# Spreading seven routing steps over later row blocks in a fused MoE and attention kernel

## The chip, the cores and the metric

The kernel runs on one core of one Trainium2 chip. The metric is the device time of one execution in microseconds (us). Three executions of the kernel before took 2537.6, 2530.3 and 2535.9 us; their median is 2535.9 us.

## The reference

Two transformer blocks run one after the other on 512 tokens of width 1024. The first has a convolution mixer and then a layer of 16384 experts. For each token and each of 8 heads the layer finds the 16 best experts (two top-16 searches over 128 scores each, then a top-16 over the 256 sums of the winners), and each chosen expert is one row of `u` (a dot product with the token) and one row of `v` (added to the token, weighted):

```python
v1, i1 = lax.top_k(s1, 16)
v2, i2 = lax.top_k(s2, 16)
cand = (v1[..., :, None] + v2[..., None, :])
vals, pos = lax.top_k(cand, 16)
idx = i1[pos // 16] * 128 + i2[pos % 16]
gates = softmax(vals)
act = gelu(einsum("chkd,cd->chk", u[idx], xc))
out = einsum("chk,chkd->cd", act * gates, v[idx])
```

The second block is: a feed-forward layer (hidden width 2816), two attention mixers over the same tokens with gated outputs, and a second feed-forward layer.

## The kernel before, in words

**Rows.** The tokens lie in 4 tiles of 128. A "row" of the kernel is one expert choice for one tile: 4 tiles x 8 heads x 16 choices = 512 rows. For a row, GpSimd issues a gather (L2104) that brings one `u` row and one `v` row for each of the 128 tokens into one of 7 pair buffers (1 MB). VectorE makes the dot product (`dot`, L1519), ScalarE the gelu and the weight (L1593). The `v` half is added in one of two ways: for most of rows 0 to 263 by a diagonal matmul on TensorE (L551), and for all rows from 264 on by VectorE (`add_row`, L963, two rows behind the dot). A buffer is free for the gather of row i when row i - 7 has been added.

**Blocks and routing.** 16 rows, those of one tile and one head, are a block, n = 0 to 31. The indices and gates of a block come from `route(n)` on VectorE: 21 pieces (three top-16 searches, the sums, the decoding of positions), which a Python generator hands out, 4 pieces after each row's dot and add, so that one route is spread over 6 rows. `ROUTES[n]` lists which routes are made while block n's rows are worked on. A second route of a block begins 8 rows after the first. After a route, ScalarE takes its exponentials (`gates(r)`, three instructions), six rows after the route's first. There are 16 slots for finished routes. GpSimd waits for route n before the first gather of block n.

**Chains.** Tiles 0 and 1 are ready after row 255. From then on the whole second block of the model for these 256 tokens ("chain A") is worked on beside rows 256 to 511; TensorE has nothing else from row 264 on. Chain A's stages are a norm, feed-forward 1 (22 weight chunks up, 12 down), a norm, the projections (`lat`, `fq`, `fk`, `fv`), 32 attention steps (`look`, `turn`, `prep`), the gates and branches, a norm, and feed-forward 2. After row 511 the same second block follows for tiles 2 and 3 ("chain B").

**Order.** Every engine works in program order. On VectorE, ScalarE and GpSimd the steps of chain A are put between the rows by a fixed table: `clock(i)` gives each row a time (`PACE`, L98), each step of the chain has a planned time, and behind row i come the steps that are due. A step that is not yet ready so holds up the rows behind it on its engine. VectorE's loop is

```python
for n in range(32):
    for k in range(16):
        if k % 8 == ROUTE_AT[n]:
            steps = route(ROUTES[n][k // 8]) if k // 8 < len(ROUTES[n]) else iter(())
        i = 16 * n + k
        dot(i)
        if i >= 2 and not ON_PE[i - 2]:
            add_row(i - 2)
        for _ in range(4):
            next(steps, None)
        ...
        first.until(clock(i))
```

Weights come in chunks of up to 1 MB through three buffers, issued by SyncE; a buffer is filled again when TensorE has used it.

Of the kernel before, what the change touches and what calls it, by code (L numbers as in the profile page):

```python
# [114 lines left out]
ON_PE = [i < HALF + 8 and not (i < 128 and i % 4 == 3) for i in range(PAIRS)]  # L115

ROUTES, SLOTS = [], 16
for _k in [1] * 8 + [2] * 8 + [1, 2, 1, 2, 1] + [0] * 11:
    _at = 1 + sum(len(r) for r in ROUTES)
    ROUTES.append(list(range(_at, _at + _k)))  # L120

ROUTE_AT = [2 if _n < 8 else 0 for _n in range(32)]
UP_TO = [(sum(ON_PE[:i]), i - sum(ON_PE[:i])) for i in range(PAIRS + 1)]
# [2121 lines left out]
```

## Time and profile before

| | |
|---|---|
| median of 3 runs | 2535.9 us |
| profiled execution, time | 2537.6 us |
| profiled execution, span of its instructions | 2535.8 us |
| TensorE busy | 84% |
| VectorE busy | 71% |
| ScalarE busy | 46% |
| GpSimd busy | 29% |
| HBM traffic | 760.86 MB, 300 GB/s on average |

Busy shares are averages over stages of very different kinds. From about 250 to 1870 us the rows are worked on, from 965 us together with chain A; from 1876 us to the end chain B runs alone.

### The profile page before, as it was taken

The numbers are of one execution on the slowest core, as the hardware profiler recorded it, in microseconds if no ns is written. First come the engines' busy times: TensorE is split into PE (matmuls) and PEld (weight loads), VectorE is DVE, ScalarE is ACT, GpSimd is POOL, SyncE is SP. The second block draws the span as 40 slices with busy tenths as digits, with TensorE's granted clock in tenths as the row PEclk, the third lists the DMA queues.
The fourth block names the chain that finished last, engine by engine and source line by source line (L and its number), as shares of the span: only waits on it lengthen the run. The fifth ranks groups of instructions, "written<-read, shape, count | busy, mean of one in ns | idle before, by whom it ended". The sixth has DMA issues, their size and how long they took to land.

```text
span 2535.8 us, 28491 instructions
## 1 busy us (share of the span) xinstructions
PE 2139.5 (84%) x9496; PEld 1516.8 (60%) x9496; DVE 1812.1 (71%) x3312; ACT 1178.1 (46%) x3774; POOL 745.8 (29%) x634
## 2 busy tenths in 40 slices
PE   6987898988777778998755697999739989998999
PEld 6965443433222227873434484786339977797997
DVE  6975767778888887888898968675665546546454
ACT  5224555656666664432455543333244435344442
POOL 0002344454554543233555533332310002000000
PEclk9988999999999998999866598999969989799999
DMA  5112999999999998999998999999945542124453
GB/s 208 67 67 97 392 390 413 412 421 421 421 421 420 416 408 343 399 420 395 370 364 319 369 420 421 376 421 421 378 188 188 185 148 88 67 99 167 160 189 133
DMA packets 107458, 760.86 MB, mean 300 GB/s; under 512 B 12064, under 2 KB 12832, under 8 KB 16432
## 3 DMA queue, kind: packets, MB, share of 16 engines
q0 software_dynamic: 73728, 536.90, 52.1%
q1 hardware_dynamic: 33584, 222.15, 23.1%
q8 instruction: 75, 1.23, 0.2%
q14 instruction: 71, 0.58, 0.1%
HBM read 756.91 MB, written 2.10 MB: 299 GB/s over the span
## 4 chain that ended last, share of the span: by engine, by line
PE 42%; DVE 9%; DMA 5%; issue 3%; ACT 2%; POOL 1%; DVEq 0%; ACTq 0%
PE bank L551 41%; DMA pair<-in_uv,idx 5%; DVE resid L963 4%; DVE pair L1519 2%; DVE half L957 1%; DVE tmp L957 1%; PE bank L923 0%; PE bank L571 0%; ACT frow L1593 0%; ACT half L1593 0%; DVE smalls L1236 0%; POOL pair L2104 0%; DVE smalls L1309 0%; POOL smalls L2059 0%; DVE ft_lo L957 0%
## 5 line engine op out<-in xcount | busy, mean ns | idle before, releaser
L2104 POOL DMA_INDIRECT pair<-in_uv,idx x512 | 641.7, 1253 | 901.5 <-DVE resid L963 573.1
L1593 ACT ACTIVATE smalls<-smalls 128x1 f32<-128x1 f32 x2058 | 540.2, 286 | 669.3 <-DVE smalls L1519 651.0
L1519 DVE CUSTOM_DVE_ANT_0 pair<-pair,hn 128x1024 f32<-128x1024 f32 x512 | 623.5, 1219 | 174.8 <-DMA pair<-in_uv,idx 173.1
L551 PE MATMUL bank<-pair,diag 128*128 128x512 f32 x928 | 459.3, 627 | 120.2 <-ACT diag L1593 119.4
L551 PEld LDWEIGHTS bank<-pair,diag 128*128 128x128 f32 x928 | 168.5, 194 | 392.7 <-ACT diag L1593 247.1
L551 PE MATMUL bank<-ft,raw 128*128 128x256 f32 x1664 | 365.7, 383 | 11.9 <-DVE ft L957 11.9
L963 DVE SCALAR_TENSOR_TENSOR resid<-pair,smalls,resid 128x1024 f32<-128x1024 f32 x280 | 358.1, 1279 | 0.6 <-ACT smalls L1593 0.3
L551 PEld LDWEIGHTS bank<-ft,raw 128*128 128x128 f32 x1664 | 320.3, 193 | 57.2 <-issue 12.7
L957 DVE TENSOR_TENSOR half<-raw,half 128x1024 fp32r<-128x1024 f32 (+1 forms) x204 | 235.0, 1193 | 136.3 <-ACT half L1593 136.3
L551 PE MATMUL bank<-ft_hi,half 128*128 128x256 f32 x1664 | 299.0, 282 | 6.4 <-DVE ft_lo L957 6.4
L1593 ACT ACTIVATE half<-raw 128x1024 fp32r<-128x1024 f32 (+1 forms) x204 | 199.7, 1029 | 153.9 <-PE bank L551 145.9
L551 PEld LDWEIGHTS bank<-ft_hi,half 128*128 128x128 f32 x1664 | 258.0, 190 | 7.2 <-DVE ft_lo L957 7.2
L551 PE MATMUL bank<-ft_lo,half 128*128 128x256 f32 x832 | 234.5, 282 | 0.0
L551 PEld LDWEIGHTS bank<-ft_lo,half 128*128 128x128 f32 x832 | 158.4, 190 | 0.0
L551 PE MATMUL bank<-raw,hidden 128*128 128x512 f32 x352 | 151.4, 592 | 0.0
L1593 ACT ACTIVATE smalls<-smalls,gat 128x1 f32<-128x1 f32 x512 | 143.2, 280 | 0.0
L551 PE MATMUL bank<-ht,raw 128*128 128x512 f32 (+2 forms) x320 | 126.7, 540 | 0.7 <-ACT ht L1593 0.7
L2034 POOL TENSOR_TENSOR smalls<-smalls,mh 128x1 f32<-128x1 f32 (+1 forms) x21 | 14.2, 682 | 377.8 <-DVE smalls L960 377.5
L1593 ACT ACTIVATE fsg<-bank 128x256 f32<-128x256 f32 x88 | 33.4, 380 | 193.5 <-PE bank L551 193.4
L551 PEld LDWEIGHTS bank<-raw,hidden 128*128 128x128 f32 x352 | 66.9, 190 | 83.3 <-issue 83.2
L551 PE MATMUL bank<-half,hidden_hi 128*128 128x512 f32 x352 | 110.3, 394 | 1.6 <-DVE half L957 1.6
L571 PE MATMUL bank<-idt,frow 128*128 128x128 f32 x96 | 22.2, 424 | 99.1 <-ACT frow L1593 99.1
(256 smaller groups left out, 2709.3 us busy)
## 6 DMA issues: line engine op xcount, KB each, us to landing
raw<-in_wts SPq DMA_DIRECT2D x196, 1024.0 KB, 6.1
pair<-in_uv,idx POOLq DMA_INDIRECT x512, 11.2
raw<-in_wts SPq DMA_DIRECT2D x10, 512.0 KB, 6.2
raw<-in_wts SPq DMA_DIRECT2D x4, 720.0 KB, 6.2
resid<-in_x SPq DMA_DIRECT2D x4, 512.0 KB, 6.7
out<-resid SPq DMA_DIRECT2D x8, 256.0 KB, 5.7
raw<-in_wts SPq DMA_DIRECT2D x2, 768.0 KB, 7.1
rowt<-in_rows SPq DMA_DIRECT2D x1, 1076.0 KB, 12.4
```

The costliest lines, as they stand in the source:

```text
L551: return e.matmul(o, a, b, start=start, stop=stop)
L571: ins = e.transpose(o[:, j * P:j * P + n], src[0:n, kt * P:(kt + 1) * P], idt[0:n, 0:n])
L957: return e.tensor_tensor(o, a, b, op)
L963: return e.scalar_tensor_tensor(out=o, in0=a, scalar=s, in1=b, op0=op0, op1=op1)
L1519: e.tensor_tensor_reduce(b[:, 0:1024], b[:, 0:1024], HN[i // 128], 1.0, 0.0, ALU.mult, ALU.add, actv[:, i % 8:i % 8 + 1]).then_inc(dotted, 1)
L1593: return e.activation(o, i, f, **kw)
L2034: e.tensor_tensor(nrs[0:n, c:c + 1], nqs[0:n, c:c + 1], mh[0:n, 0:1], ALU.pow).then_inc(n_rs, 1)
L2104: e.indirect_dma_start(pair[i % NPAIR], None, uv, bass.IndirectOffsetOnAxis(ap=idx[:, n % SLOTS, k:k + 1], axis=0)).then_inc(pairs_in[i % ...
```

## The change

Routes 1 to 24 stay where they are, in blocks 0 to 15. Routes 25 to 31 were made in blocks 16 to 20 as 1, 2, 1, 2, 1. They are now made one to a block in blocks 18 to 24.

```diff
 ROUTES, SLOTS = [], 16
-for _k in [1] * 8 + [2] * 8 + [1, 2, 1, 2, 1] + [0] * 11:
+for _n in range(32):
     _at = 1 + sum(len(r) for r in ROUTES)
-    ROUTES.append(list(range(_at, _at + _k)))
+    ROUTES.append(list(range(_at, min(32, _at + (1 if _n < 8 else 2 if _n < 16 else 0 if _n < 18 else 1)))))
```

| block | 16 | 17 | 18 | 19 | 20 | 21 | 22 | 23 | 24 |
|---|---|---|---|---|---|---|---|---|---|
| routes before | 25 | 26, 27 | 28 | 29, 30 | 31 | | | | |
| routes after | | | 25 | 26 | 27 | 28 | 29 | 30 | 31 |

## Rows read from the trace of the kernel before

**Rows 1.** The page: busy us and share of the span of each engine.
```profile
PE 2139.5 (84%) x9496; PEld 1516.8 (60%) x9496; DVE 1812.1 (71%) x3312; ACT 1178.1 (46%) x3774; POOL 745.8 (29%) x634
```

**Rows 2.** Windows with L1519 alone; each row's dot is two instructions there.
```profile
core 0: us, DVE busy (x), PEclk, DMA share, GB/s
0.00:925.30 925.30, 313.29 (x512) 0.95 0.81 330
...
965.00:1195.00 230.00, 68.09 (x112) 0.99 0.98 393
...
1236.20:1449.00 212.80, 79.49 (x129) 0.67 0.93 360
```

**Rows 3.** Windows by stage: length, engines' busy time, clock, DMA share, GB/s.
```profile
core 0: us, PE busy (x) PEld busy (x) DVE busy (x) ACT busy (x) POOL busy (x), PEclk, DMA share, GB/s
925.00:948.00 23.00, 17.12 (x36) 5.99 (x35) 21.14 (x53) 14.69 (x58) 11.28 (x11) 1.00 1.01 413
...
965.00:1119.00 154.00, 153.98 (x704) 135.28 (x705) 129.79 (x270) 60.56 (x229) 47.29 (x42) 0.99 0.98 389
1119.00:1195.00 76.00, 75.84 (x178) 33.37 (x176) 60.53 (x127) 22.03 (x93) 22.03 (x19) 1.00 0.99 402
...
1291.00:1351.00 60.00, 31.06 (x83) 17.36 (x83) 49.98 (x87) 31.12 (x127) 30.74 (x21) 0.55 0.85 327
...
1236.00:1449.00 213.00, 133.78 (x450) 82.95 (x449) 190.56 (x318) 121.14 (x483) 118.83 (x86) 0.67 0.93 360
1594.00:1748.00 154.00, 153.79 (x705) 135.15 (x706) 102.77 (x141) 55.21 (x223) 52.26 (x47) 0.99 0.98 402
```

**Rows 4.** Timeline of PE, 950 to 1230 us: start, length, instructions, idle before.
```profile
965.02 154.29 PE L551 MATMUL bank<-ft,raw 128*128 128x256 f32 x704 [6.65 <-DVE ft L957]
1119.14 75.70 PE L551 MATMUL bank<-raw,hidden 128*128 128x512 f32 x176
1213.91 3.67 PE L571 MATMUL bank<-idt,frow 128*128 128x128 f32 x16 [19.07 <-ACT frow L1593]
```

**Rows 5.** Timeline of PE in feed-forward 2 of chain A.
```profile
1594.21 153.72 PE L551 MATMUL bank<-ft,raw 128*128 128x256 f32 x704 [5.28 <-DVE ft L957]
```

**Rows 6.** Chain that ended last, in order of time, 900 to 1500 us.
```profile
965.02 228.12 PE bank L551 x876
...
1194.99 1.20 DVE resid L963
...
1304.28 1.21 DVE pair L1519
```

**Rows 7.** Waits of DVE, 1236 to 1449 us: total, times, longest.
```profile
DVE smalls L1309 <- PE bank L551: 9.2, 3, 6.7
DVE smalls L957 <- ACT lat L1593: 6.9, 1, 6.9
DVE ym L957 <- PE bank L551: 4.5, 1, 4.5
DVE qm L957 <- POOL smalls L2059: 2.5, 3, 1.4
DVE tmp L957 <- ACT fq L1593: 2.4, 1, 2.4
```

**Rows 8.** Timeline of DVE: three of these waits at their places.
```profile
1236.14 0.18 DVE L957 TENSOR_TENSOR smalls<-lat,rowt 128x16 f32<-128x16 f32 x1 [6.89 <-ACT lat L1593]
...
1246.50 0.69 DVE L957 TENSOR_TENSOR tmp<-fq 128x512 f32<-128x512 f32 x1 [2.35 <-ACT fq L1593]
...
1358.00 0.42 DVE L1309 TENSOR_REDUCE smalls<-bank 128x1 f32<-128x256 f32 x1 [1.91 <-PE bank L551]
```

**Rows 9.** Windows 804 to 884 us, DVE, by tile: vals, cand, ohb, idx (four routes).
```profile
804.00:884.00 80.00, 14.99 (x68) 1.00 1.01 416
...
804.00:884.00 80.00, 11.03 (x36) 1.00 1.01 416
...
804.00:884.00 80.00, 8.41 (x12) 1.00 1.01 416
...
804.00:884.00 80.00, 0.68 (x4) 1.00 1.01 416
```

**Rows 10.** Groups of DVE, same stretch: busy us, mean ns, idle before.
```profile
L957 DVE TENSOR_TENSOR cand<-vals 128x256 f32<-128x256 f32 x4 | 1.7, 425 | 0.1
...
L960 DVE TENSOR_SCALAR pu<-pu 128x16 uint32<-128x16 uint32 x8 | 1.0, 169 | 0.0
```

**Rows 11.** ACT instructions of `gates`, by tile: ns min/median/max.
```profile
L1593 ACT ACTIVATE gat<-gat,sm x32: 307/308/310, 241.3 to 1203.4; 128x16 f32<-128x16 f32 x32
```

## The prediction

> **What bounds the kernel now.** I read the page first. VectorE (DVE) is busy 71% of the span, TensorE (PE) 84% [rows 1]; neither number says what a route costs, because a route costs time only in a stretch where VectorE sets the pace. So the questions are which rows the routes sit beside before and after, what time of the trace those rows are, and who sets the pace there.
>
> To turn rows into times I count dots in the windows. Before 925.3 us there are 512 instructions of L1519, two a row, so row 256 (block 16) starts there. Between 965 and 1195 us there are 56 dots, and from 1236.2 to 1449 us 64.5 [rows 2]: 1236.2 us is the start of row 336 (block 21) and 1449 us is the start of block 25. The four blocks that gain a route, 21 to 24, are thus exactly the stretch 1236 to 1449 us. Blocks 16, 17 and 19 lose one, two and one; blocks 18 and 20 have one route before and after, under another number.
>
> Then the pace. *Feed-forward 1 of chain A, 965 to 1195 us.* The timeline of PE shows 704 matmuls in one piece of 154.3 us and 176 in one piece of 75.7 us, with no idle time between or inside [rows 4], and the chain that ended last runs 228.12 us on PE alone from 965.02 us [rows 6]. VectorE is busy 129.8 of 154 us there and 60.5 of 76 us [rows 3]: it has room. *Projections and attention, 1236 to 1449 us.* PE is busy 133.8 of 213 us with much of that at a low granted clock (0.55 of full speed, near the lower of its two levels, in 1291 to 1351 us), the DMA engines moved 360 GB/s (327 in the middle of it, against 413 to 416 where they are full), and VectorE is busy 190.6 of 213 us, 89% [rows 3, 9]; here the chain runs over dots and adds [rows 6]. VectorE sets the pace. So the change moves four routes from stretches that other engines set into one that VectorE sets.
>
> **One route.** In 804 to 884 us four routes run. By tile, VectorE's work on vals, cand, ohb and idx is 14.99 + 11.03 + 8.41 + 0.68 us [rows 9]; the sums of winners name both vals and cand and are taken off once (1.7), the two shifts of positions are added (1.0) [rows 10]: 34.4 us for four, 8.6 us each. Idle time inside is about 0.1 us a group, so I leave it.
>
> **What leaves blocks 17 and 19 (three routes, 25.8 us of VectorE).** In feed-forward 1 VectorE waits for PE's results in fixed order, so less work gives a longer wait. PE's piece of 154.3 us has no gap that VectorE could have caused. The trace has a control for it: feed-forward 2 of chain A is the same 704 matmuls beside rows with no route at all. There VectorE is busy 102.8 instead of 129.8 us, and PE takes 153.7 us instead of 154.3 [rows 3, 5]. I take the gain as 0; the control allows 0.6.
>
> What the Trainium skill says speaks against this reading: "Perfetto Trace Analysis", section Identifying the Most-Contended Engine, warns that matmul busy time is not a fair measure of how near PE is to its limit, and has the reader use the weight loads' busy time instead. By that, PEld at 135.28 of 154 us (88%) would leave 18.7 us of room in this stage, and the sum below would come out 18.7 us lower. The control speaks against it in this case, and the rival below has its price from rows.
>
> **What leaves block 16 (one route, 8.6 us).** Rows 256 to 261. In 925 to 948 us VectorE is busy 21.1 of 23 us, but the DMA engines are full, at 413 GB/s [rows 3]; a row is 1 MB, and 23 us at 416 instead of 413 GB/s [rows 9] would be 0.2 us shorter. No weights are loaded there, so the gathers are the limit a little under VectorE. Bounds: 0 and 8.6 us gained. I take 1, near the DMA row.
>
> **What comes into blocks 21 to 24 (four routes, 34.4 us).** Each is on rows 0 to 5 of its block, 4 pieces a row. It is free only where VectorE now waits for something that the route does not itself delay. VectorE's waits in this stretch are 22.4 us (213 - 190.6) [rows 3], of which the waits with a name are 9.2, 6.9, 4.5, 2.5 and 2.4 us [rows 7]. One by one:
> - 6.9 us for lat ends at 1236.14 us [rows 8], before row 336: ahead of the first inserted piece, so nothing is absorbed.
> - 2.35 us for fq at 1246.50 us [rows 8], behind row 338. Twelve pieces of route 28 come ahead of it, over 2.35 us of work: absorbed whole.
> - 1.91 us at 1358.00 us [rows 8], behind row 369. Eight pieces of route 30 come ahead: absorbed whole.
> - The longest of the 9.2 us (6.7, at row 364) and the 4.5 us (row 399) stand after the route of their block has ended (rows 357 and 389). They are round trips VectorE to PE and ScalarE and back that start after it: they move with it and absorb nothing. So do the 2.5 us for POOL.
> - Small waits of 0.4 to 0.6 us: I give them 1 in all.
>
> So 34.4 - 2.35 - 1.91 - 1 = 29.1 us are added. If everything behind the first wait were absorbed, 22.4 - 6.9 = 15.5 us, it would be 18.9; if nothing, 34.4.
>
> **What moves with the routes.** On ScalarE the three instructions of `gates` follow each route, the longest 0.31 us [rows 11]; 4 times under 0.7 us, under 3 us, beside 121 busy of 213 us [rows 3]. They are hidden by ScalarE's waits for dots; uncovered they cost up to 2.8. GpSimd's half of the gates is tied to the block that uses them and does not move; nor does any gather or weight load. No wait is new: route 31 is now ready at row 389 and first needed by the gather of row 496; slots of 16 are free long before. What is late next: everything behind row 336 on VectorE, with it the adds that free pair buffers, the attention steps, and so the start of the gate stage on PE at 1449 us. From there on the order is unchanged, the pair buffers are as full as before (no route in rows 390 to 399), and nothing gives time back: feed-forward 2 is PE's, chain B starts after row 511.
>
> **The sum.** -1 (block 16) + 0 (17 and 19) + 29.1 (21 to 24) = +28, against the profiled execution's 2537.6 us: about 2566. The median is 1.7 us below that execution, so 2564 on the median.
>
> **The rivals.**
> *A, the gaps swallow more.* All waits behind row 336 take in route work (15.5 us instead of 5.3). For it: PE also waits in attention, so the loop through PE and ScalarE may have a pace of its own. Against: the longest waits stand where no route precedes them. Gives +18.9 - 1 = +18, 2554; with all of block 16's route gained as well, +10, 2546.
> *B, feed-forward 1 is not PE's.* Then its stage shrinks to what DMA allows: 154 us at 389 and 76 us at 402 GB/s are 90.5 MB [rows 3], at 416 GB/s 217.5 us, so -12.5 us; against it the control. Gives +28 - 12.5 = +15.5, about 2551.
> *C, the other side: VectorE sets feed-forward 1 too, DMA included.* Each of the four routes taken out then gives its 8.6 us, 34.4, against 29.1 put in: -5, 2531. It decides once more than 29.1 us are gained before row 336, which DMA alone forbids by the arithmetic of B unless block 16 gives its whole 8.6 and DMA can run faster than any stretch shown. That the routes weigh the same in both places (within 0.3% either way) is its weaker form.
> *D, it costs more.* Nothing is absorbed, the gates lie open and round trips stretch because pieces of a route stand between the attention step and its answer: 34.4 + 2.8 = +37, 2573.
> That the change does not do what it says is excluded: the order is fixed when the program is built.
>
> **How the numbers follow.** Forecast, +22 to +34: 0.66. A 0.11, B 0.06, C 0.04 and its weaker form 0.04, D 0.09. The range 2549 to 2573 takes in the forecast, most of A, B and D. A measurement of this kernel tells about 0.3% (8 us) from no change; the chance of slower by more is 0.92, within it 0.04, faster 0.04 (C alone; its price of -5 is itself inside 8 us, but a C that holds at all would not stop at the bound that DMA sets).
>
> **What would show it.** In the trace after: PE's pieces in feed-forward 1 still 154 and 76 us, starting at about 964 us, with VectorE's busy time there 26 us lower and its waits for fsg and for the down bank longer; the 64 rows of blocks 21 to 24 in 242 us instead of 213, with VectorE busy over 92%; the waits at rows 338 and 369 gone and those at rows 364 and 399 still there; from the gate stage on all as before, 28 us later. The prediction is wrong if PE's 154 us shrink, if the attention blocks lengthen by under 20 us, or if the rows behind block 25 make up time because the DMA backlog of that stage (gathers beside new weights) is smaller when it starts later.

## The result and the profile after

The changed kernel is slower by 1.0%: 2556.05 us median (2554.14 to 2564.01, 4 runs) against 2534.44 us for the kernel before in the same comparison; the ratio is 1.0099, with a 95% interval of 1.0084 to 1.0114, which is 25 us. The ratio is not that of these two medians, which lie 21.6 us apart: of the changed kernel 21 executions are on record, with a median of 2558.66 us. The forecast was 2564 us and 28 us slower. The profiled execution took 2555.7 us with a span of 2553.9 us, so the two profiles differ by 18 us only. 5.5 us of the missing time lie before row 256, where the two kernels are the same: over all ten profiles of this study row 256 starts between 919.9 and 929.0 us. I therefore compare stages, not ends.

First the windows by stage of the kernel after, at the bounds that answer to those of before (same columns as [rows 3]):

```profile
958.60:1113.30 154.70, 154.66 (x705) 135.81 (x706) 117.92 (x218) 56.66 (x224) 49.95 (x43) 0.98 0.99 401
1113.30:1189.00 75.70, 75.58 (x177) 33.13 (x175) 48.34 (x86) 20.28 (x85) 23.93 (x18) 1.00 0.96 389
...
1288.00:1355.60 67.60, 31.56 (x85) 17.59 (x83) 57.84 (x118) 31.74 (x130) 27.68 (x21) 0.53 0.78 288
...
1228.80:1467.10 238.30, 137.72 (x447) 85.79 (x445) 220.59 (x441) 123.04 (x494) 109.98 (x86) 0.62 0.86 324
```

Feed-forward 1 (the first two lines) takes 154.7 and 75.7 us as before, though VectorE, the third busy time, has 11.9 and 12.2 us less to do there. Blocks 21 to 24 (the last line) take 238.3 us; VectorE is busy 220.6 of them, 93% instead of 89%, and the DMA engines moved 324 GB/s instead of 360. The line before it is block 22 alone.

The timeline of PE has the same two pieces, the first 0.4 us longer than before and the second equal, and the chain of waits again runs over PE alone there [rows 4, 6]:

```profile
958.64 154.71 PE L551 MATMUL bank<-ft,raw 128*128 128x256 f32 x704 [6.68 <-DVE ft L957]
1113.18 75.70 PE L551 MATMUL bank<-raw,hidden 128*128 128x512 f32 x176
1207.95 3.67 PE L571 MATMUL bank<-idt,frow 128*128 128x128 f32 x16 [19.08 <-ACT frow L1593]
```

```profile
958.64 228.54 PE bank L551 x876
```

What VectorE had saved became waiting. First its waits in feed-forward 1 before, 965 to 1195 us, then after, 958 to 1189 us (total, times, longest):

```profile
DVE hidden L957 <- ACT fsg L1593: 19.0, 12, 5.5
DVE resid L963 <- PE bank L551: 11.5, 2, 10.4
DVE pair L1519 <- DMA pair<-in_uv,idx: 5.7, 7, 1.3
```

```profile
DVE hidden L957 <- ACT fsg L1593: 35.3, 18, 5.9
DVE resid L963 <- PE bank L551: 25.6, 2, 18.6
DVE pair L1519 <- DMA pair<-in_uv,idx: 1.3, 1, 1.3
```

The three together go from 36.2 to 62.2 us: 26.0 us more, and three routes are 25.8.

The waits of VectorE in blocks 21 to 24 after, which answer to [rows 7]:

```profile
DVE smalls L1309 <- PE bank L551: 6.7, 1, 6.7
DVE smalls L957 <- ACT lat L1593: 5.4, 1, 5.4
DVE ym L957 <- PE bank L551: 4.5, 1, 4.5
DVE qm L957 <- POOL smalls L2059: 2.3, 2, 1.4
```

The 2.4 us for fq is gone, and of the 9.2 us on PE's bank only the single 6.7 us is left. The waits of 6.7, 4.5 and 1.4 us are as long as before; why no inserted piece shortens them is shown under gaps.

The stages, by the starts of the dots (rows) and of PE's pieces in both traces:

| stretch | before | after | difference | forecast |
|---|---|---|---|---|
| row 256 to PE's up piece | 39.6 | 38.7 | -0.9 | -1 |
| PE's up and down pieces | 229.8 | 230.3 | +0.5 | 0 |
| to row 336 | 41.4 | 39.9 | -1.5 | 0 |
| block 21 | 54.8 | 59.2 | +4.4 | |
| block 22 | 60.2 | 67.6 | +7.4 | |
| block 23 | 47.9 | 53.9 | +6.0 | |
| block 24 | 49.1 | 57.6 | +8.5 | |
| blocks 21 to 24 | 212.0 | 238.3 | +26.3 | +29.1 |
| block 25 to the end | 1087.5 | 1086.8 | -0.7 | 0 |
| from row 256 on | 1610.4 | 1634.0 | +23.6 | +28 |

One profile of a kernel is not exact to a microsecond. In the five other profiles without a route in blocks 21 to 24 and without idle sums there (late, late2, ffn1, pad_ffn1, pad2_ffn1) these blocks take 211.0 us, 1.0 less than in the profile before, which has two waits of 0.26 and 0.38 us for gathers at rows 350 and 351 that the others lack. Against 211.0 us the four routes cost 27.3 us instead of 26.3.

### The profile page after: what moved, and what is told of

Its sections match the earlier page's. It is cut to its first block, busy times and chain, and to the rows that moved or that the text cites. A ratio compares the mean times of both kernels' runs of the same rounds, so it can differ in the third digit from the quotient of the medians.

```text
span 2553.9 us, 28487 instructions
## 1 busy us (share of the span) xinstructions
PE 2139.1 (84%) x9496; PEld 1517.1 (59%) x9496; DVE 1811.9 (71%) x3312; ACT 1174.6 (46%) x3770; POOL 760.2 (30%) x634
## 4 chain that ended last, share of the span: by engine, by line
PE 42%; DVE 12%; DMA 5%; issue 3%; ACT 1%; POOL 0%; DVEq 0%; ACTq 0%
PE bank L551 40%; DVE resid L963 5%; DMA pair<-in_uv,idx 4%; DVE pair L1519 3%; DVE half L957 1%; PE bank L923 1%; DVE tmp L957 1%; PE bank L571 0%; DVE smalls L1236 0%; ACT frow L1593 0%; ACT half L1593 0%; DVE smalls L1309 0%; DVE ft_lo L957 0%; DVE ohb L957 0%; DMA raw<-in_wts 0%
## 5 line engine op out<-in xcount | busy, mean ns | idle before, releaser
L2104 POOL DMA_INDIRECT pair<-in_uv,idx x512 | 651.3, 1272 | 905.8 <-DVE resid L963 601.6
L1519 DVE CUSTOM_DVE_ANT_0 pair<-pair,hn 128x1024 f32<-128x1024 f32 x512 | 623.8, 1220 | 169.8 <-DMA pair<-in_uv,idx 168.7
L1593 ACT ACTIVATE half<-raw 128x1024 fp32r<-128x1024 f32 (+1 forms) x204 | 199.7, 1029 | 154.8 <-PE bank L551 146.7
```

The lines of the kernel that those rows point to most:

```text
L1519: e.tensor_tensor_reduce(b[:, 0:1024], b[:, 0:1024], HN[i // 128], 1.0, 0.0, ALU.mult, ALU.add, actv[:, i % 8:i % 8 + 1]).then_inc(dotted, 1)
L1593: return e.activation(o, i, f, **kw)
L2104: e.indirect_dma_start(pair[i % NPAIR], None, uv, bass.IndirectOffsetOnAxis(ap=idx[:, n % SLOTS, k:k + 1], axis=0)).then_inc(pairs_in[i % ...
```

## The experiments

The routes of an experiment are given as the list for blocks 16 and on; the kernel before has 1, 2, 1, 2, 1 and the changed one 0, 0, 1, 1, 1, 1, 1, 1, 1. All ratios are to the kernel before, with 95% intervals.

**late: the four routes in blocks 25 to 28 instead of 21 to 24.**

```diff
-for _k in [1] * 8 + [2] * 8 + [1, 2, 1, 2, 1] + [0] * 11:
+for _k in [1] * 8 + [2] * 8 + [0, 0, 1, 1, 1, 0, 0, 0, 0, 1, 1, 1, 1, 0, 0, 0]:
```

> Routes 25, 26, 27 in blocks 18, 19, 20 as in the changed kernel, routes 28 to 31 in blocks 25 to 28 (gates, branches, start of feed-forward 2) instead of 21 to 24. Theory (a route costs time only beside the projections and attention, where VectorE sets the pace): about 2536 us, 2530 to 2545, so some 20 us under the changed kernel (2556), with blocks 21 to 24 back at 212 us. Rival (routes cost because they are made late, or because they leave feed-forward 1): 2550 us or more.

Measured 2542.73 us, ratio 1.0039 (1.0024 to 1.0054): 10 us over the kernel before and, by the ratios, 15 under the changed one; from row 256 on the two profiles are 6.0 us apart. Blocks 21 to 24 are back at 211.0 us. But block 25 takes 57.2 instead of 54.0 us, block 26 takes 59.0 instead of 55.0, and the 36.9 us from row 432 to feed-forward 2 become 40.2; feed-forward 2 itself is unchanged (its up piece is 154.1 us). The theory's direction holds and its price for the new places was too low. In the windows of this kernel's blocks 25 and 26

```profile
1444.10:1501.20 57.10, 56.91 (x259) 50.06 (x260) 46.05 (x80) 23.60 (x93) 20.65 (x18) 0.97 0.93 371
1501.20:1560.30 59.10, 44.22 (x157) 32.20 (x156) 54.48 (x105) 24.18 (x93) 19.99 (x18) 0.86 1.00 408
```

VectorE is busy 54.5 of 59.1 us in block 26: a route fills the room there and goes over it. Block 25 is not explained so: VectorE is busy only 46.1 of 57.1 us there and still waits 9.3 us for gathers (13.6 in the kernel before), yet the block takes 3.2 us more. Why is not shown.

**late2: the same four in blocks 27 to 30.** The line that is added, in place of the line with 1, 2, 1, 2, 1:

```diff
+for _k in [1] * 8 + [2] * 8 + [0, 0, 1, 1, 1, 0, 0, 0, 0, 0, 0, 1, 1, 1, 1, 0]:
```

> As late, but routes 28 to 31 in blocks 27 to 30, beside feed-forward 2 of chain A, instead of 25 to 28. Theory (feed-forward 2 is TensorE's, as feed-forward 1; what late lost, 3 to 4 us in each of blocks 25, 26 and 27, was lost in the gate and branch stage and at the norm): the stage's two TensorE pieces stay 154 and 76 us; block 27 still loses 3 us; about 2536 us (2531 to 2540). Rival (any late route costs some 2.5 us, wherever it is): 2543 us as late.

Measured 2538.94 us, ratio 1.0011 (0.9998 to 1.0023), so a loss is not clear of the noise. The three routes beside feed-forward 2 are free; this is its timeline of PE:

```profile
1582.37 3.68 PE L571 MATMUL bank<-idt,frow 128*128 128x128 f32 x16 [17.61 <-ACT frow L1593]
1591.08 154.28 PE L551 MATMUL bank<-ft,raw 128*128 128x256 f32 x704 [5.03 <-DVE ft L957]
1745.19 75.70 PE L551 MATMUL bank<-raw,hidden 128*128 128x512 f32 x176
```

PE's pieces are 154.3 and 75.7 us [rows 5]. The one in block 27 stands ahead of the norm: row 432 to the start of feed-forward 2 takes 42.0 instead of 36.9 us, 5.1 us more, where I had said 3. The rival (any late route costs, 2543 us) is out, since the interval ends at 2540.5 us: a route made at row 480 costs less than one made at row 352.

**double: all seven in blocks 21 to 24.** The line that is added:

```diff
+for _k in [1] * 8 + [2] * 8 + [0, 0, 0, 0, 0, 2, 2, 2, 1] + [0] * 7:
```

> All seven routes in blocks 21 to 24 (2, 2, 2, 1), none in 16 to 20. Theory: blocks 21 to 24 take 7 x 7.5 us of VectorE's net time minus some 5 us of absorbed waits more, about 260 instead of 212 us; block 16 gives 1 us, block 20 some 3 us; about 2578 us, 2568 to 2585. Rival (attention's round trips have a pace of their own and swallow routes): blocks 21 to 24 stay near the 238 us of the changed kernel, 2560 us or less. Rival (a route weighs the same wherever it is): 2534 us.

Measured 2582.56 us, ratio 1.0190 (1.0175 to 1.0206), 48 us. Blocks 21 to 24 take 259.5 us, of which

```profile
1233.00:1492.50 259.50, 136.55 (x447) 84.47 (x445) 244.42 (x534) 125.39 (x504) 105.11 (x86) 0.63 0.82 296
```

VectorE is busy 244.4. Seven routes are 60.2 us by [rows 9, 10], and 47.5 of them show: 6.8 us a route, where four give 26.3, 6.6 a route. The three that come on top of the changed kernel's four cost 21.2 us, 7.1 each. It does not level off, so attention has no pace of its own below VectorE's. Block 24 with its one route is 57.6 us in both.

**gaps: the routes of blocks 22 and 24 begin at row 7 of the block.** Against the changed kernel:

```diff
-ROUTE_AT = [2 if _n < 8 else 0 for _n in range(32)]
+ROUTE_AT = [2 if _n < 8 else 7 if _n in (22, 24) else 0 for _n in range(32)]
```

> The changed kernel with the routes of blocks 22 and 24 begun at row 7 of the block instead of row 0, so that route 29 (rows 359 to 364) stands inside the round trip that ends in VectorE's 6.7 us wait at row 364. Theory (a wait absorbs pieces that stand inside its round trip and none that stand before it): the 6.7 us wait shrinks by 2 to 4 us, the 4.5 us wait at row 399 stays; about 2553 us, 2550 to 2555. Rival (ScalarE's and TensorE's half of the round trip is held up by the pieces too, since they wait for dots): no change from 2556.

Measured 2560.10 us, ratio 1.0101 (1.0086 to 1.0117), that of the changed kernel. My expectation failed: with pieces of route 29 on every row from 359 to 364, the wait at row 364 is

```profile
1351.67 0.29 DVE L1309 TENSOR_REDUCE smalls<-bank 128x1 f32<-128x128 f32 x1 [6.59 <-PE bank L551]
```

6.59 us instead of the 6.68 of the changed kernel. The two waits for POOL at row 360 (1.44 and 0.85 us) are filled, and block 22 is 66.1 instead of 67.6 us, but not this one. The 4.5 us wait at row 399 stays, as expected.

The traces show the reason: I had put the start of the round trip too early. In all ten profiles, whatever the routes, this wait ends 9.09 to 9.10 us after the start of row 364's dot. The trip starts with VectorE's sum L1309, 0.2 us ahead of that dot; ScalarE takes it up within 0.05 us of its end, and in the kernel before PE's projection follows 1.45 us after the dot's start and runs for 6.35 us:

```profile
1329.89 0.28 DVE L1309 TENSOR_REDUCE smalls<-bank 128x1 f32<-128x128 f32 x1
1330.09 1.21 DVE L1519 CUSTOM_DVE_ANT_0 pair<-pair,hn 128x1024 f32<-128x1024 f32 x1
1330.21 0.37 ACT L1593 ACTIVATE rowt<-bank,smalls 128x128 f32<-128x128 f32 x1 [0.22 <-DVE smalls L1309]
1331.54 6.35 PE L551 MATMUL bank<-raw,qlt 128*128 128x384 f32 x8 [7.13 <-ACT qmt L1593]
```

So only work between that dot and the wait is inside the trip. In gaps that is the last piece of the route alone (0.17 us), and the wait is 0.09 us shorter. In double a second route runs on rows 360 to 365, four of its pieces stand behind dot and add of row 364, and the wait falls by 2.34 us, to

```profile
1360.46 0.29 DVE L1309 TENSOR_REDUCE smalls<-bank 128x1 f32<-128x128 f32 x1 [4.34 <-PE bank L551]
```

In pad_att (below) one sum of 0.60 us stands there, and the wait is 6.08 us. The rule of this experiment (a wait takes in what stands inside its round trip and nothing ahead of it) holds. Its rival had the number that came (no change), but by a mechanism that is not there: that the pieces hold up the other engines' part of the trip is out, as it takes the same 9.1 us each time.

**ffn1: 1, 2, 2, 2 in blocks 16 to 19, none behind.** The line that is added:

```diff
+for _k in [1] * 8 + [2] * 8 + [1, 2, 2, 2, 0] + [0] * 11:
```

> Seven routes in blocks 16 to 19 (1, 2, 2, 2), none in block 20 or later: against the kernel before, one route goes from rows 320 to 325 (around the end of feed-forward 1) into feed-forward 1 proper. Theory (feed-forward 1 is TensorE's): TensorE's pieces stay 154 and 76 us; the last five pieces of route 31, behind VectorE's wait for the down bank at row 323, give 2.5 us; about 2532 us (2528 to 2535). Rival (VectorE sets feed-forward 1): 5 to 8 us slower, about 2541.

Measured 2533.62 us against 2533.63, ratio 1.0002 (0.9991 to 1.0014). PE's pieces take 154.8 and 75.7 us with a sixth route beside them (the seven of this kernel less route 25, which is made before they start). From the end of the down piece to row 336 it is 38.7 instead of 41.4 us; I had said 2.5 less. How much of the 2.7 us is the route's is not certain: seven profiles of kernels with one route in block 20 (all but pad2_ffn1) take 39.8 to 42.8 us there, and the two without such a route 38.7 and 38.9. A gain of 0.1% is inside the interval of the whole time, so this kernel is not shown to beat the one before.

**pad_ffn1 and pad2_ffn1: how much room feed-forward 1 has.** One idle sum behind each of 32 rows in pad_ffn1, two in pad2_ffn1, whose edit this is (pad_ffn1 has `1 if`):

```diff
+                    for _ in range(2 if 272 <= i < 304 else 0):
+                        mine()
+                        e.tensor_reduce(spare, HN[3][:, 0:512], X, ALU.add).then_inc(v_step, vs_.up())
```

> The kernel before with one more instruction on VectorE behind each of rows 272 to 303: a sum over 512 elements that nobody uses, some 0.69 us, 22 us in all, inside feed-forward 1. VectorE waits some 18 us in these rows and 10.4 us at row 313. Theory (TensorE's stage): 0 to 4 us more, about 2536 us. Rival (VectorE sets feed-forward 1): 22 us more, 2556 us.

> As pad_ffn1 with two such instructions a row, 44 us in all. This looks for the end of the room: the last hidden tiles then come later than TensorE's up piece ends. Theory: the room in these rows is some 20 us, what is over it delays the down piece; about 20 us more, 2554 us (2545 to 2562). Rival (VectorE sets it): 44 us more, 2578 us. Rival (there is no edge near): 2536 us.

One a row: 2534.61 us, ratio 1.0002 (0.9988 to 1.0016). By the starts of the instructions it is 19 us more work rather than the 22 I had said (see pad_att), and nothing in the time; PE's up piece is 154.7 us. Two a row, 41 us more work: 2549.17 us, ratio 1.0068 (1.0041 to 1.0094), 17 us. Here the timeline of PE has the edge:

```profile
961.67 153.89 PE L552 MATMUL bank<-ft,raw 128*128 128x256 f32 x704 [6.68 <-DVE ft L958]
1115.40 35.35 PE L552 MATMUL bank<-raw,hidden 128*128 128x512 f32 x82
1155.02 42.91 PE L552 MATMUL bank<-raw,hidden 128*128 128x512 f32 x94 [4.26 <-DVE hidden L958]
1226.70 3.68 PE L572 MATMUL bank<-idt,frow 128*128 128x128 f32 x16 [28.77 <-ACT frow L1597]
```

The up piece is not touched even now (153.9 us). The down piece breaks in two with a wait of 4.26 us for VectorE's hidden tile and takes 82.5 instead of 75.7 us, and the norm behind it comes 28.8 instead of 19.1 us after it. This is what a late VectorE looks like in this stage, and the kernel after has no trace of it. The rule that the forecast weighed ("Perfetto Trace Analysis" of the Trainium skill, section Identifying the Most-Contended Engine: judge TensorE's distance from its limit by its share of peak FLOPs and its weight-load time, not by matmul busy time) was read in the forecast as 18.7 us to be had in this stage from a lighter VectorE; that is an estimate from the rule, which does not itself say that a lighter VectorE gives them. VectorE's load went up by 19 us (pad_ffn1) and its busy time down by 24 us (the change) without shortening or breaking the up piece, which disagrees with using the rule so here: PEld was busy 88% and PE was nevertheless the pace.

**pad_att: the same 32 sums, one a row, behind rows 352 to 383** (`1 if 352 <= i < 384`).

> The kernel before with the same 32 instructions behind rows 352 to 383 (blocks 22 and 23, attention), 22 us in all. Theory (VectorE sets this stage; the small waits of 1.9 and some 2 us are absorbed, the 6.7 us one is not): 17 to 20 us more, about 2552 us. Rival (attention's round trips have a pace of their own): 10 us more or less.

Measured 2545.30 us, ratio 1.0051 (1.0038 to 1.0064), 13 us (the medians are 10.7 us apart); blocks 22 and 23 take 66.1 and 55.5 instead of 60.2 and 47.9 us, +13.5. The same work that is free in feed-forward 1 costs 13 us here. It is less than the 17 to 20 I had said, and lies between that and the rival's 10; double above speaks against the rival's pace of attention's own, and most of what is missing here can be named. In the groups of this kernel

```profile
L1569 DVE TENSOR_REDUCE smalls<-hn 128x1 f32<-128x512 f32 x32 | 21.7, 677 | 0.0
```

the sum's record is 677 ns, but the next instruction starts about 0.08 us before that record ends; in the timeline from 1289.87 us the next dot starts 0.60 us after the sum, so the work added is 32 x 0.60 = 19.2 us. The waits in these two blocks give back 4.2 us of it: 9.2 + 2.5 us in the kernel before, and in this kernel 6.9 + 0.6 us,

```profile
DVE smalls L1310 <- PE bank L552: 6.9, 2, 6.1
DVE qm L958 <- POOL smalls L2063: 0.6, 1, 0.6
```

The remaining 1.5 us between 19.2 - 4.2 = 15.0 and 13.5 have no named row.

## Why the prediction was right, point by point

**Who sets the pace.** Shown. Feed-forward 1 is PE's: with less VectorE work (the change, double) and with more (ffn1, pad_ffn1), PE's up piece stays between 154.0 and 155.0 us and its down piece at 75.7; only pad2_ffn1 moves the down piece. Blocks 21 to 24 are VectorE's: one, two or no routes and idle sums all move them. Rival B (feed-forward 1 shrinks to what DMA allows) and rival C (it is VectorE's) are both out; C's point of decision, over 29.1 us gained before row 336, is far from the 1.9 us that the profile shows (0.9 - 0.5 + 1.5), of which the 1.5 us lie in a stretch that takes 39.8 to 42.8 us in profiles of kernels with the same routes there.

**Block 16.** -1 forecast, -0.9 in the profile; the other four kernels that take route 25 out of block 16 (late, late2, double and gaps) also show 38.7 instead of 39.6 us. The reason given, that gathers are the limit a little under VectorE, is borne out by VectorE's waits for them from row 256 to the up piece, which grow from 2.5 to 10.0 us. Before, then after:

```profile
DVE pair L1519 <- DMA pair<-in_uv,idx: 2.5, 3, 1.2
```

```profile
DVE pair L1519 <- DMA pair<-in_uv,idx: 10.0, 8, 1.3
```

**One route.** 8.6 us by its pieces. In the kernel after, the steps from the start of each route instruction to the start of the next instruction add up to 34.4 us for the four, the forecast's term to a tenth.

**What the waits absorb.** This term was too small. The two that I named, 2.35 us at row 338 and 1.91 us at row 369, are gone, and those at rows 364 and 399 stand, as said; the reason given for them, a round trip that starts behind the route, is right, and double shows its limit, since a route that reaches past row 364's dot does shorten the wait there. But the idle time of VectorE over 0.1 us within blocks 21 to 24 fell from 21.2 to 14.7 us, by 6.5 and not by 5.3; the rest is 0.2 to 0.6 us waits, which I had given 1 us in all. A further 1.6 us between 34.4 - 6.5 = 27.9 and the measured 26.3 I can't give to a named row: VectorE's 316 other instructions are as many and as long as before, but their starts stand 1.4 us closer together in all, waits left out. So the step that was mis-sized is the 29.1 us, which measured 26.3, for want of 2.8 us of absorption; against the 211.0 us of the five other profiles it measured 27.3 and the want is 1.8 us. Rival A (15.5 us absorbed) and D (nothing absorbed) were on both sides of it.

**Behind block 25.** Nothing is given back: -0.7 us over 1087 us. The doubt that the DMA backlog of the gate stage would shrink was empty; blocks 25 and 26 take 53.9 and 55.0 us, as before.

**Gates, gathers, slots.** The sum gave them nothing, and no stretch of the table calls for more.

## What to carry to other kernels

Where several engines work through one fixed order, give each stretch of the order its owner before moving work: find in the trace the engine without gaps, and look for a control, the same stage elsewhere with more or less of the work in question. Work of another engine is free beside its owner up to the length of that engine's waits (here waits of 36 us in 230: 19 us more were free, and 41 us more broke the stage at its hand-over, not in the middle), and costs most of its length in a stretch that it owns itself: 6.6 to 6.8 of 8.6 us here. To fill a wait at the end of a round trip, put the work behind the instruction that starts the trip; ahead of it, it only shifts the trip. Spreading work evenly over time is no gain in itself; a lighter load in a stage that others pace only turns into a longer wait.

## What the runs showed of the hardware that was not expected

Some of VectorE's records overlap: in pad_att the instruction behind an idle sum starts about 0.08 us before the sum's record ends, so 32 instructions of 677 ns were 19.2 us and not 21.7 us of added work. It is not so everywhere: where pad2_ffn1 has two such sums in a row, the second starts 0.035 us after the record of the first ends, and 64 of them were 41 us. So the price of an added instruction is read from the starts of its neighbours, not from its record.
